# Four expert pieces loaded in requests of 112 rows and a few rows each, in place of 128 rows

## The reference, cut to what matters

```python
def expert_choice_ffn(h, w_router, w1, w3, w2):      # D = 1024, F = 2048, E = 16
    cap = EC_CAPACITY * L // N_EXPERTS               # 32 tokens for each expert
    aff = jax.nn.softmax((h @ w_router).astype(jnp.float32), axis=-1)
    gate, idx = lax.top_k(jnp.swapaxes(aff, 1, 2), cap)
    xe = h[b_idx, idx]
    a = jnp.einsum('becd,edf->becf', xe, w1)
    u = jnp.einsum('becd,edf->becf', xe, w3)
    y = jnp.einsum('becf,efd->becd', jax.nn.silu(a) * u, w2)
    y = y * gate[..., None].astype(y.dtype)
    return jnp.zeros_like(h).at[b_idx, idx].add(y)
```

## Time and profile before

| | us |
|---|---|
| median of 3 runs | 1375.07 |
| the profiled execution | 1374.77 |
| its span, first to last instruction | 1372.9 |
| TensorE busy | 1060.3 |
| VectorE busy | 479.6 |
| ScalarE busy | 283.7 |

### The profile page before, as it was taken

One profiled execution on the slowest core, in us unless ns is written; L12 is line 12 of the kernel. 1 busy time (PEld: TensorE's weight loads), 2 busy tenths in 40 slices (PEclk: granted clock), 3 DMA queues, 4 the chain that ended last, 5 costly groups with the idle time before them and its releaser, 6 DMA issues.

```text
span 1372.9 us, 16739 instructions
## 1 busy us (share of the span) xinstructions
PE 1060.3 (77%) x7266; PEld 622.3 (45%) x7266; DVE 479.6 (35%) x897; ACT 283.7 (21%) x498; POOL 57.7 (4%) x83
## 2 busy tenths in 40 slices
PE   9999999999999997475667758577475665657576
PEld 7977886799977833131321313223131231313223
DVE  5977777887887312010110101101010110101113
ACT  6536655653355200000000000000000000000002
POOL 0005300000000000000000000000000000000000
PEclk9999999999999998777877877877777878778779
DMA  9755168444535999999999999999999999999996
GB/s 377 275 208 209 58 220 353 188 154 171 196 125 208 410 416 438 433 434 432 432 427 432 434 434 431 433 433 433 432 427 432 432 436 430 432 432 434 434 420 258
DMA packets 21136, 487.14 MB, mean 355 GB/s; under 512 B 2535, under 2 KB 3080, under 8 KB 4936
## 3 DMA queue, kind: packets, MB, share of 16 engines
q1 hardware_dynamic: 20200, 484.51, 83.8%
q10 hardware_dynamic: 864, 1.57, 0.3%
HBM read 485.02 MB, written 1.05 MB: 354 GB/s over the span
## 4 chain that ended last, share of the span: by engine, by line
DMA 44%; PE 43%; DVE 10%; issue 1%; ACT 1%; POOL 1%; SPq 0%; DVEq 0%; ACTq 0%
DMA places<-in_experts 42%; PE ps L280 41%; DVE xT L1778 2%; DMA ring<-in_pieces 1%; DVE ring_r L334 1%; DVE R L1746 1%; DVE R L1742 1%; DVE sm L1395 0%; PE ps L1790 0%; ACT ring_r L328 0%; POOL hT L792 0%; POOL hT L794 0%; DVE ring L608 0%; DVE U_r L537 0%; PE ps L1418 0%
## 5 line engine op out<-in xcount | busy, mean ns | idle before, releaser
L280 PE MATMUL ps<-places,R 128*32 128x512 f32 (+2 forms) x3168 | 463.1, 746 | 264.3 <-DMA places<-in_experts 262.3
L280 PEld LDWEIGHTS ps<-places,R 128*32 128x32 f32 x3168 | 112.3, 135 | 594.1 <-DMA places<-in_experts 302.3
L1739 DVE SCALAR_TENSOR_TENSOR R<-R,ps 128x512 f32<-128x512 f32 x16 | 11.0, 688 | 303.3 <-ACT R L1734 303.3
L280 PE MATMUL ps<-hT_r,ring_r 128*128 128x256 f32 x400 | 113.1, 283 | 0.0
L280 PE MATMUL ps<-U_r,ring_r 128*128 128x256 f32 x480 | 107.7, 284 | 0.4 <-DVE hT_r L525 0.3
L334 DVE TENSOR_TENSOR ring_r<-ring,ring_r 128x2048 fp32r<-128x2048 f32 (+1 forms) x44 | 98.7, 2274 | 25.0 <-ACT ring_r L328 24.9
L1742 DVE SCALAR_TENSOR_TENSOR R<-R,ps 128x512 f32<-128x512 f32 x16 | 11.0, 688 | 231.6 <-PE ps L280 231.6
L280 PE MATMUL ps<-late_r,ring_r 128*128 128x256 f32 x448 | 84.4, 286 | 1.2 <-DVE U_r L537 0.9
L328 ACT ACTIVATE ring_r<-ring 128x2048 fp32r<-128x2048 f32 (+1 forms) x44 | 81.7, 1896 | 7.0 <-DMA ring<-in_pieces 7.0
L280 PEld LDWEIGHTS ps<-U_r,ring_r 128*128 128x128 f32 x480 | 82.1, 192 | 1.2 <-DVE hT_r L525 1.0
L280 PEld LDWEIGHTS ps<-hT_r,ring_r 128*128 128x128 f32 x400 | 76.6, 192 | 0.7 <-issue 0.5
(11 more groups left out here) (355 smaller groups left out, 1094.4 us busy)
## 6 DMA issues: line engine op xcount, KB each, us to landing
places<-in_experts SPq DMA_DIRECT2D x54, 6144.0 KB, 49.6
places<-in_experts SPq DMA_DIRECT2D x29, 2048.0 KB, 17.4
ring<-in_pieces SPq DMA_DIRECT2D x20, 2048.0 KB, 8.6
ring<-in_wmodt SPq DMA_DIRECT2D x8, 2048.0 KB, 8.4
ring<-in_wmodk SPq DMA_DIRECT2D x4, 2048.0 KB, 8.6
ring<-in_pieces SPq DMA_DIRECT2D x2, 1024.0 KB, 7.2
places<-in_experts SPq DMA_DIRECT2D x2, 1024.0 KB, 33.2
ring<-in_pieces SPq DMA_DIRECT2D x1, 1792.0 KB, 11.9
```

The source lines that it names most:

```text
L280: mm = lambda e, o, l, r, st, sp_=True, sk=False: e.matmul(o, l, r, start=st, stop=sp_, skip_group_check=sk)
L1739: e.scalar_tensor_tensor(h, h, 1.0, bank[2 * (ex % 2)][:, :], ALU.add, ALU.mult).then_inc(s["me_h2"], 1)
```

## The change

The pieces 12, 13, 14 and 15 are loaded in several requests of whole rows, one behind the other, in place of one request of 128 rows. Each piece begins with a request of rows 0 to 111; rows 112 to 127 follow in two or three requests: 8, 4 and 4 rows for piece 12, 14 and 2 for piece 13, 12 and 4 for piece 14, 10 and 6 for piece 15. The bytes are the same and lie in the same places. The value that says that a piece is there counts 16 for each request. All other pieces are loaded as before.

```diff
+    ROWS = {12: (112, 8, 4, 4), 13: (112, 14, 2), 14: (112, 12, 4), 15: (112, 10, 6)}
     MOE_LOADS = {}
     n = [SLOT_LOADS[i] if i < NSLOT else 0 for i in range(NMOE)]
     for q in range(193):
         if moe_first(q) == q:
-            n[moe_sem(q)] += 16
+            n[moe_sem(q)] += 16 * len(ROWS.get(q, (128,)))
         MOE_LOADS[q] = n[moe_sem(q)]
...
         src, at = moe_src(q)
         n = SLOT if q < 191 else SLOT // 2
-        e.dma_start(slots[moe_slot(q)][:, 0:n], src[:, at:at + n]).then_inc(slot_sem[moe_sem(q)], 16)
+        a = 0
+        for r in ROWS.get(q, (128,)):
+            e.dma_start(slots[moe_slot(q)][a:a + r, 0:n], src[a:a + r, at:at + n]).then_inc(slot_sem[moe_sem(q)], 16)
+            a += r
```

## The result

The changed kernel takes 1396.40 us (median of 4 runs, 1394.72 to 1398.84); the kernel before, run beside it on the same chip, 1374.97 (4 runs, 1374.55 to 1375.25). The ratio is 1.0162, 95% interval 1.0149 to 1.0175: 21.4 us slower, where +12 was predicted and +20 was the top of the likeliest case. The profiled execution has a span of 1397.0 us, 24.1 more than before.

The account below looks back on a forecast made before the run. The DMA engines' time for the bytes was taken to bound the kernel from piece 12 on. First engines: 17.0 + 19.4 = 36.4 against 19.4 us, 17.0 back, less 5.0 lead: +12, 1387 us; range 1374.5 to 1396.

Parts of the forecast that it names:

- the likeliest case: Write paths bind for the split requests of pieces 12 to 15: +12 us (from +4 to +20), chance 0.63.
- The bound: From piece 12 on, the time is what the DMA engines need for the bytes at 432 GB/s; TensorE doesn't set it.
- Rows per engine: In pieces 12 to 15, 112-row requests give each engine 28 rows, 17.0 us; before, 32 rows, 19.4 us.
- Write paths bind small requests: In the nine requests on rows 112 to 127: 2.4 us each for 4 rows or more, 1.2 us for 2.
- Clashes in the requests of 112 rows add 0 or more: In the 112-row requests an engine's 7 rows need no longer lie on a path of its own: 0 or more.
- The average lead of 5.0 us taken off: At the end of the loads, engines average 5.0 us ahead of the last, so 17.0 us becomes +12.
- The signs to look for: DMA share near 1 at 250 to 350 GB/s in 480 to 505 us; loads' end over some 20 us; middle 432.
- worse clashes: Rival: in 112-row requests several engines meet on one path throughout; end 25 to 50 us later, 1400 to 1425; chance 0.08.
- engines only: Rival: write paths have room for the small requests, so only rows per engine count; middle 1375 us; chance 0.29.
- The turning point between the cases: Engines only decides if a four-row request takes under about 1 us, nine rows costing the first engines under 6.6 us.
- Issues on SyncE: Nine more issues on SyncE, 0.30 to 0.67 us each, hidden in its waits on TensorE: cost 0.
- TensorE and the slots: Pieces land up to 17 us later, delaying TensorE and SyncE's next issues; TensorE's idle time catches up: cost 0.

Follow-up runs that it names:

- rows0_63: Kernel before, but pieces 12 to 15 load rows 0 to 63 alone, other rows left out: 1374.36 us against 1374.20 (ratio 1.0002).
- rows32_95: Kernel before, but pieces 12 to 15 load rows 32 to 95 alone, other rows left out: 1365.01 us against 1374.20 (ratio 0.9932).
- only112: Kernel before, but pieces 12 to 15 load rows 0 to 111 alone, rows 112 to 127 left out: 1386.66 us against 1374.20 (ratio 1.0096).
- one_piece: Kernel before with only piece 12 split (112, 8, 4 and 4 rows), pieces 13 to 15 in one request each: 1378.56 us against 1374.25 (1.0036).

## Why the prediction was right and wrong

- **The bound**: right. From piece 12 on the time is the DMA engines' time for the bytes; 24.3 us of transfer lost move the average engine's end by 24.0 us and the last one's by 22.1.
- **Rows per engine**: right in the number of engines of each request, by the steps of the semaphore (35, 34, 34, 34). The Trainium skill, page "DMA: Bandwidth & Descriptors", section "Why a DMA increments its semaphore by 16 and not by 1", gives the rule, and the counts agree with it; that it is the lowest-numbered engines no run here shows.
- **Write paths bind small requests**: right in kind and near in size (a median of 2.5 us a row where 2.4 was taken for a request of four; 21.6 us where 19.4). The page "SBUF — State Buffer" of the Trainium skill, section "Door 1: The DMA port swizzle", says which partitions share a port; *rows0_63* at 213 GB/s and *rows32_95* at 370, both in 480 to 490 us, agree.
- **"Clashes in the requests of 112 rows add 0 or more"**, taken as 0: this is the step that failed. They cost 14.9 us by *only112*. The whole loss is 21.4 us and that of *only112* 12.5, so the few rows add some 9 us on top (both prices are known to some 4 us). The 0 was the end of a range with no upper end worked out, and a sum in step gives a mean of 0.80 us a row for 112 rows, 4 x 7 x (0.80 - 0.607) = 5.4 us: it could have been made once the reading of the paths was settled. It would have been 9.5 short all the same. Even more simply, by that reading rows 0 to 63 put 8 rows on each of eight paths, which makes 4 x 8 x 0.607 = 19.4 us at the least, where the prediction had 17.0.
- **The average lead of 5.0 us taken off**: wrong. It was meant for two engines that fall back among others. Here all did (22.0 to 24.2 us at piece 16), and what the engines' lead gave back at the end is 1.9 us (24.0 against 22.1), in *one_piece* 1.2. Without it the sum would have been +17.0. Nor may 17.0 and 14.9 be added to 31.9: by the runs the 112-row requests alone lose 12.5 us and the few rows add some 9. Why these 9 are less than 17.0 was not tested; the few rows may be written while other engines are held up in 112-row requests anyway.
- **The signs to look for**: the share near 1 and the unchanged middle came; the rate was lower than the 250 to 350 foretold (216 over 50 us) and low for 50 us, not 25; the end drawn out to 20 us did not come. TensorE idle behind 500 us and over 20 us lost were named as the mark of worse clashes, and both came. The end spread of 8.3 us was named as a mark of engines only; it is not one, since all engines fell back together.
- **The rivals**: engines only is out. Worse clashes, given 0.08 and 1400 to 1425 us, has the right mechanism for most of the loss: engines meet on the paths all through the 112-row requests. Its price was put too high, since a meeting of all at twice the time was its least case (+17.0 by itself, on top of the rest), while *only112*, at 1.18 us a row, gives 14.9. The prediction's reason against it, that the loads of 128 and of 64 rows keep the engines apart, is wrong for the 64 rows and at odds with its own reading of them, half of the paths for sixteen engines: *rows0_63* needs 1.27 us a row. The truth lies between the two cases, 0.4 us above the range.
- **The turning point between the cases**: worked out wrong. The first engines stay within the 9 us if the nine rows cost under 19.4 + 9 - 17.0 = 11.4 us, not 17.0 + 9 - 19.4 = 6.6. No chance was worked out from it in numbers, and the rows cost more than either.
- **Issues on SyncE**: cost 0, right. Pieces 12 to 15 go out within 0.12 us of before; the one late by 0.59 us is covered, the DMA share being 1.06 in 485 to 490 us.
- **TensorE and the slots**: cost 0, right as far as the loads go. TensorE is idle for most of some 20 us, but only as long as the loads are behind, and has caught up: the window from 1000 to 1100 us is again at 432 GB/s, with 66.5 us of TensorE in it. The 2.0 us behind the last load, in the profiled execution, were in no term.

## What to carry to other kernels

Where a load binds, ask of each request not only how many engines it uses but which rows they write at the same moment: a request of 128 rows keeps the sixteen apart, one of 112 or of 64 rows from row 0 on ran at half the rate here. Price such clashes before the balance between engines: the first was worth some 15 us in this kernel, the second 5 at the very best. And take a lead of some engines off the sum only if it is shown that the others aren't held back too.

## What the runs showed of the hardware beyond what was expected

- 64 rows can be loaded at nearly the full rate or at half of it: in 480 to 490 us rows 32 to 95 at 370 GB/s (the kernel before has 390 there), rows 0 to 63 at 213.
- Requests that are each on separate paths still meet with other pieces' requests in the queue: seven engines with seven rows each ran at 0.611 us a row alone, and with the nine others at later pieces all sixteen needed 1.1 to 1.3 us.
- Above some 11 engines with seven neighbouring rows each the total doesn't grow: 229, 257, 210 and 229 GB/s for 9, 11, 13 and 16.
- A DMA issue on SyncE, 0.24 to 0.41 us otherwise, took 1.39 us at 487.39 when twelve others had gone out in 8 us, and 5.6 and 9.0 us at 502.65 and 508.30. None of the twelve issues of single pieces from 479 us on in the kernel before took over 0.33.
